# A recurrent head's outputs kept with tokens on partitions, its gate applied at once, and the sample states' decay on ScalarE

## What is computed

```python
h = rms_norm(x, norm1)
u, q, f, i, g = split(h @ w_in)             # 5 parts of 1024 columns
pool_out = pool_mix(u)                      # 4 groups, trailing windows 2, 4, 8, 16
# 8 heads of 128: forget gate F, key 1 - F, query silu(q), value i
F = lb + (1 - lb) * sigmoid(f)
S_t = diag(F_t) S_{t-1} + (1 - F_t)^T v_t   # a 128 x 128 state for each head and sequence
o_t = silu(q_t) S_t
o = rms_norm(o over the head's 128) * hg_norm * silu(g)
x = x + concat(pool_out, o) @ w_o
x = x + (silu(h2 @ w_gate) * (h2 @ w_up)) @ w_down      # h2 = rms_norm(x), width 5632
y = rms_norm(x)
```

## Time and profile before

| | us |
|---|---|
| median of 3 runs | 1520.35 (1520.12 to 1521.35) |
| the profiled execution: its own time | 1519.69 |
| its span, first to last instruction | 1517.9 |
| mean granted clock of TensorE | 0.981 of full speed |
| busy: PE, weight loads, VectorE, ScalarE, GpSimd | 1463.0, 1441.3, 792.6, 560.7, 239.3 |

### The profile page before, as it was taken

How to read it: one execution, slowest core, us unless ns; L and a number is a source line. 1 busy time by engine, 2 the same in 40 slices (tenths; PEclk the granted TensorE clock), 3 DMA queues, 4 the chain that set the end, 5 groups by cost and what they waited for, 6 DMA issues and landing times.

```text
span 1517.9 us, 26905 instructions
## 1 busy us (share of the span) xinstructions
PE 1463.0 (96%) x9816; PEld 1441.3 (95%) x9816; DVE 792.6 (52%) x1214; ACT 560.7 (37%) x831; POOL 239.3 (16%) x410
## 2 busy tenths in 40 slices
PE   7998989889989999999999999999999999999996
PEld 5998988889979999999999999999999999999996
DVE  4556776666755555544444444444444444544443
ACT  6443434434333334333333333333333333333343
POOL 0265345454502220000000000000000000000131
PEclk9999999998989999999999999999999999999998
DMA  8554434445435555554555554556555456555453
GB/s 228 143 133 127 115 97 126 118 134 139 114 100 136 141 152 149 141 154 132 141 162 158 151 153 130 145 149 168 154 139 156 128 145 177 141 155 149 114 142 118
DMA packets 409519, 214.58 MB, mean 141 GB/s; under 512 B 4093, under 2 KB 407757, under 8 KB 409420
## 3 DMA queue, kind: packets, MB, share of 16 engines
q1 hardware_dynamic: 391207, 203.59, 49.2%
q10 hardware_dynamic: 18277, 10.52, 2.4%
HBM read 206.20 MB, written 7.89 MB: 141 GB/s over the span
## 4 chain that ended last, share of the span: by engine, by line
PE 83%; DVE 6%; POOL 4%; issue 3%; ACT 2%; DMA 1%; ACTq 0%; DVEq 0%; POOLq 0%; SPq 0%
PE bank L383 26%; PE bank L384 26%; PE bank L385 26%; POOL km L1555 2%; DVE qr L1224 1%; POOL kp L1564 1%; DVE w_lo L1039 1%; ACT w_hi L695 1%; PE bank L523 1%; DVE sc L1239 1%; DMA xt<-in_x_sample 1%; PE bank L551 0%; PE bank L479 0%; DVE sn L1283 0%; DVE t L1211 0%
## 5 line engine op out<-in xcount | busy, mean ns | idle before, releaser
L383 PE MATMUL bank<-a_hi,w_hi 128*128 128x320 f32 x2048 | 645.4, 315 | 0.0
L384 PE MATMUL bank<-a_lo,w_hi 128*128 128x320 f32 x2048 | 638.9, 312 | 0.0
L385 PE MATMUL bank<-a_hi,w_lo 128*128 128x320 f32 x2048 | 638.7, 312 | 0.0
L1039 DVE TENSOR_TENSOR w_lo<-w_raw,w_hi 128x1024 fp32r<-128x1024 f32 (+1 forms) x416 | 460.0, 1146 | 161.3 <-ACT w_hi L695 159.9
L695 ACT ACTIVATE w_hi<-w_raw 128x1024 fp32r<-128x1024 f32 (+1 forms) x416 | 387.2, 967 | 164.7 <-PE bank L385 137.9
L383 PEld LDWEIGHTS bank<-a_hi,w_hi 128*128 128x128 f32 x2048 | 390.2, 191 | 2.5
L384 PEld LDWEIGHTS bank<-a_lo,w_hi 128*128 128x128 f32 x2048 | 390.4, 191 | 0.8
L385 PEld LDWEIGHTS bank<-a_hi,w_lo 128*128 128x128 f32 x2048 | 390.0, 190 | 0.0
L383 PE MATMUL bank<-h_hi,w_hi 128*128 128x320 f32 x704 | 217.7, 309 | 0.0
L384 PE MATMUL bank<-h_lo,w_hi 128*128 128x320 f32 x704 | 216.5, 308 | 0.0
L385 PE MATMUL bank<-h_hi,w_lo 128*128 128x320 f32 x704 | 216.5, 308 | 0.0
(11 more groups left out here) (228 smaller groups left out, 1245.3 us busy)
## 6 DMA issues: line engine op xcount, KB each, us to landing
w_raw<-in_w_gate SPq DMA_DIRECT2D x44, 1024.0 KB, 5.6
w_raw<-in_w_up SPq DMA_DIRECT2D x44, 1024.0 KB, 5.6
w_raw<-in_w_down SPq DMA_DIRECT2D x64, 704.0 KB, 4.8
w_raw<-in_w_in SPq DMA_DIRECT2D x39, 1024.0 KB, 5.8
w_raw<-in_w_o SPq DMA_DIRECT2D x16, 1024.0 KB, 6.0
s<-in_state_hgrn ACTq DMA_DIRECT2D x8, 512.0 KB, 6.6
out<-sn ACTq DMA_DIRECT2D x8, 512.0 KB, 6.5
xt<-in_x_prompt SPq DMA_DIRECT2D x3, 512.0 KB, 9.2
```

What stands on the lines that cost most here:

```text
L383: pe.matmul(out, whi[:, par_, cols], r_hi, start=(k == 0), stop=False)
L384: pe.matmul(out, whi[:, par_, cols], r_lo, start=False, stop=False)
L385: last = pe.matmul(out, wlo[:, par_, cols], r_hi, start=False, stop=(k == last_k))
L1039: dve.tensor_tensor(wlo[:, par_, cols], raw[:, par_, cols], whi[:, par_, cols].bitcast(F32), SUB)\
```

## The change

Units now come as f q v g for each of the heads 0 to 4 (units `H0` to `L0`), then f q v of heads 5, 6 and 7, then g5 g6 g7. The number of units is the same. A round of the loop is f_{i+1}, q_{i+1}, v_{i+1}, g_{i+1}, four rounds; outputs start four units apart five times, and then twice three.

- `rec_out` has weights and moving side exchanged: `OT` now holds *tokens on partitions*, 128 + 128 + 64, and features as columns. In `rec_s0` a stored state is the moving side (128 columns), and the weights are a window of 32 columns of `qm`, in which only the 8 queries of that sequence aren't zero. `qm` is zeroed once by GpSimd, and VectorE writes the queries into it in `queries` (one product more; the product of level 2 loses its sample columns).
- ScalarE squares `OT` in three instructions with `accum_out`, so the sums over a head's features come out as a column per token block. It takes mean and root, then runs a dummy Silu. VectorE does reciprocal and Newton step. ScalarE scales the three blocks (`rec_scale`), and PE transposes them back (`rec_back`, 3 transposes). `rec_stat`, `rec_bcast`, the diagonals, `osb` and the intermediate split are gone.
- VectorE multiplies the turned output, `hg_norm` and silu(g) in one instruction (`rec_gate`); one split follows. For heads 5 and 6 the turned output is kept in `onb` until their gates exist.
- Silu of q and g is one ScalarE instruction each, in place of sigmoid and a GpSimd product; the forget values use Tanh.
- The decay of the sample states is eight ScalarE copies of 128x128 with a scale per partition (`decayed`); GpSimd keeps `vm`, keys and key copies.
- For the first head VectorE now waits for `sc_zero` ahead of `queries(0)`, and `pool_lo` comes ahead of it.

The diff, cut to what matters. SP's loads follow the new order of units and aren't shown, nor are semaphore names and the removed functions described above.

```diff
+L0 = H0 + 4 * EARLY
+G0 = L0 + 3 * (HEADS - EARLY)
...
+QSTEP = 40
...
             def rec_s0(r):
 
                 pe.wait_ge(s0_loaded, 16 * (r + 1))
-                after(pe, on_ready, r)
-                for b in range(NB):
-                    t = slice(TP + b * TS, TP + (b + 1) * TS)
-                    pe.matmul(OT[:, t], s0[:, b, :], qr[LS][:, t], start=(b == 0), stop=False)
+                pe.wait_ge(qm_ready, r + 1)
+                out = OT[:, TP:TP + P]
+                for i in range(HB):
+                    for j in range(2):
+                        b = HB * j + i
+                        at = QSTEP * b - TS * i
+                        pe.matmul(out[j * HS:(j + 1) * HS, :], qm[:, at:at + HS], s0[:, b, :], start=(i == 0), stop=False)
...
             def rec_out(r):
-                rec_s0(r)
+                if isinstance(r, int) and r > EARLY:
+                    pe.wait_ge(o_kept, r - EARLY)
+                else:
+                    after(pe, gated, r)
                 pe.wait_ge(s1_ready, r + 1)
                 pe.wait_ge(sc_put, PUTS * (r + 1))
-                pe.matmul(OT[:, 0:CH], vt[:, 0, :], sc[:, 0, :], start=False, stop=False)
-                pe.matmul(OT[:, CH:TP], vt[:, 1, :], sc[:, 1, :], start=False, stop=False)
-                pe.matmul(OT[:, CH:TP], s1[:, :], qr[LP][:, CH:TP], start=False, stop=False)
-                pe.matmul(OT[:, TP:N], vt[0:NS, 2, :], scs[:, :], start=False, stop=True).then_inc(o_mm, 1)
+                pe.matmul(OT[:, 0:P], sc[:, 0, :], vt[:, 0, :], start=True, stop=True)
+                pe.matmul(OT[:, P:TP], sc[:, 1, :], vt[:, 1, :], start=True, stop=False)
+                pe.matmul(OT[:, P:TP], qr[LP][:, CH:TP], s1[:, :], start=False, stop=True)
+                rec_s0(r)
+                pe.matmul(OT[0:NS, TP:TP + P], scs[:, :], vt[0:NS, 2, :], start=False, stop=True).then_inc(o_mm, 1)
...
+            def rec_back(r):
+                pe.wait_ge(o_scaled, r + 1)
+                pe.transpose(OT[:, 0:P], tm[:, 0, :], ident)
+                pe.transpose(OT[:, P:TP], tm[:, 1, :], ident)
+                pe.transpose(OT[:, TP:N], tm[0:NS, 2, :], ident[0:NS, 0:NS]).then_inc(o_back, 1)
...
+            def put_out(n, par_, r):
+
+                unit(n, par_, a_rhs, between=(lambda: rec_out(r), None))
+
+            def turned_back(n, par_, r):
+
+                unit(n, par_, a_rhs, between=(None, lambda: rec_back(r)))
...
+            scored(H0 + 3, 1, 0)
+            with pe.Fori(0, EARLY - 1) as i:
+                put_out(H0 + 4 * i + 4, 0, i)
+                turned_back(H0 + 4 * i + 5, 1, i)
+                unit(H0 + 4 * i + 6, 0, a_rhs)
+                scored(H0 + 4 * i + 7, 1, i + 1)
+            put_out(L0, 0, EARLY - 1)
+            turned_back(L0 + 1, 1, EARLY - 1)
+            unit(L0 + 2, 0, a_rhs)
+            for r in range(EARLY, HEADS - 1):
+                n = L0 + 3 * (r - EARLY) + 3
+                scored(n, n % 2, r)
+                put_out(n + 1, (n + 1) % 2, r)
+                turned_back(n + 2, n % 2, r)
+            scored(G0, 1, HEADS - 1)
+            put_out(G0 + 1, 0, HEADS - 1)
+
+            def last_back(k):
+                if k == 12:
+                    rec_back(HEADS - 1)
+            unit(G0 + 2, 1, a_rhs, after_tile=last_back)
...
+                act.activation(zf[:, :], zf[:, :], ACT.Tanh, scale=0.5).then_inc(zf_tanh, 1)
...
+                act.wait_ge(zf_tanh, h + 1)
+                act.activation(tl[0][:, :, 1:3], zf[:, :].rearrange("p (m a) -> p m a", a=2), ACT.Identity,
+                               bias=lbt[:, 3, bass.ds(h, 1)], scale=lbt[:, 5, bass.ds(h, 1)]).then_inc(f_ready, 1)
...
+            def silu_q(h, n):
                 act.wait_ge(unit_read, n + 1)
...
+                act.activation(zq[:, :], zq[:, :], ACT.Silu).then_inc(q_ready, 1)
+
+            def silu_g(g, n):
+                act.wait_ge(unit_read, n + 1)
+                after(act, gm_lo, g)
+                act.activation(ga[:, :], zf[:, :], ACT.Silu).then_inc(g_act, 1)
...
             def rec_squares(r):
                 act.wait_ge(o_mm, r + 1)
...
+                after(act, o_back, r)
+                for i in range(3):
+                    rows = P if i < 2 else NS
+                    last = act.activation(tm[0:rows, i, :], OT[0:rows, i * P:(i + 1) * P], ACT.Square,
+                                          accum_out=oss[0:rows, i:i + 1])
+                last.then_inc(o_squared, 1)
+                act.wait_ge(o_squared, r + 1)
+                after(act, o_rec, r)
+                act.activation(stat[:, 6:9], oss[:, :], ACT.Identity, bias=epst[:, 0:1], scale=1.0 / P)
+                act.activation(stat[:, 0:3], oss[:, :], ACT.Sqrt, bias=epst[:, 0:1], scale=1.0 / P).then_inc(o_std, 1)
+                act.activation(warm[:, 0:1], epst[:, 0:1], ACT.Silu)
+
+            def rec_scale(r):
+                act.wait_ge(newton_step, 4 * (r + 2))
+                for i in range(3):
+                    rows = P if i < 2 else NS
+                    last = act.activation(tm[0:rows, i, :], OT[0:rows, i * P:(i + 1) * P], ACT.Copy,
+                                          scale=stat[0:rows, 3 + i:4 + i])
+                last.then_inc(o_scaled, 1)
+
+            def decayed(r):
+
+                act.wait_ge(s0_loaded, 16 * (r + 1))
+                act.wait_ge(prod_ready, LP * (r + 1))
+                after(act, sn_stored, 16 * r)
+                for b in range(NB):
+                    m = TP // TS // 2 + b // 2
+                    last = act.activation(sn[:, b, :], s0[:, b, :], ACT.Copy, scale=tl[LS][:, m, 1 + b % 2:2 + b % 2])
+                last.then_inc(sdec_ready, 1)
 
...
+            def turn(n, h, r):
+
+                split_hi(n + 1, 1)
+                silu_g(r, n - 1)
                 rec_squares(r)
                 load_s0(h)
                 rec_stores(r)
-                sigmoid_q(h, n + 1)
-                split_hi(n + 3, 1 - par_)
-                rec_std(r)
-                rec_hi(r)
-
-            def gate_window(n, g, h, r):
-
-                split_hi(n + 1, 1)
+                forget(h, n)
+                split_hi(n + 2, 0)
+                rec_scale(r)
+                silu_q(h, n + 1)
+                split_hi(n + 3, 1)
+                gate_split(r)
+                split_hi(n + 4, 0)
+
+            def short_turn(n, h, r):
...
+                split_hi(n + 1, 1 - a)
                 rec_tokens(r)
...
+                decayed(r)
+                forget(h, n)
+                split_hi(n + 2, a)
                 rec_squares(r)
                 load_s0(h)
                 rec_stores(r)
...
+                silu_q(h, n + 1)
+                split_hi(n + 3, 1 - a)
+                rec_scale(r)
...
+            act.activation(warm[:, 0:1], epst[:, 0:1], ACT.Silu)
...
+            split_hi(H0 + 4, 0)
+            rec_tokens(0)
+            decayed(0)
+            with act.Fori(0, EARLY - 1) as i:
+                turn(H0 + 4 * i + 4, i + 1, i)
+                rec_tokens(i + 1)
+                decayed(i + 1)
...
+            n = L0
+            split_hi(n + 1, 1)
+            silu_g(EARLY - 1, n - 1)
+            rec_squares(EARLY - 1)
+            load_s0(EARLY)
+            rec_stores(EARLY - 1)
+            forget(EARLY, n)
+            split_hi(n + 2, 0)
+            rec_scale(EARLY - 1)
+            silu_q(EARLY, n + 1)
+            split_hi(n + 3, 1)
+            gate_split(EARLY - 1)
+            short_turn(L0 + 3, EARLY + 1, EARLY)
+            short_turn(L0 + 6, EARLY + 2, EARLY + 1)
...
+            silu_g(EARLY, G0)
...
+            rec_scale(HEADS - 1)
...
+                                  zq[:, :].rearrange("p (m a) -> p m a", a=2), tl[0][:, :, 1:3], MUL)\
...
+                    n = N if l < LS - 1 else TP
                     dve.wait_ge(qr_ready, (LP + 1) * h + l + 1)
+                    if l == LS - 1:
+                        dve.tensor_tensor(qm[:, :].rearrange("p (b t) -> p b t", t=QSTEP)[:, :, 0:TS]
+                                          .rearrange("p b (a j) -> p b a j", a=2),
+                                          blocks_of(qr[l][:, TP:N], l, NS), times(l, NS, 0, TP), MUL).then_inc(qm_ready, 1)
                     dve.tensor_tensor(blocks_of(qr[l + 1], l, n), blocks_of(qr[l], l, n), times(l, n, 0), MUL)\
...
+            def rec_newton(r):
+                dve.wait_ge(o_std, r + 1)
+                after(dve, o_scaled, r)
+                dve.reciprocal(stat[:, 3:6], stat[:, 0:3]).then_inc(o_rec, 1)
+                dve.wait_ge(o_rec, r + 1)
...
+            def rec_gate(r, src):
+
+                dve.wait_ge(g_act, r + 1)
+                dve.scalar_tensor_tensor(out=ga[:, :], in0=src, scalar=pcol("hg_norm", r), in1=ga[:, :],
+                                         op0=MUL, op1=MUL).then_inc(gated, 1)
+
+            def gate_lo(r):
+                dve.wait_ge(gm_hi, r + 1)
+                split_rest(bh_lo[:, r, :], ga[:, :], bh_hi[:, r, :]).then_inc(gm_lo, 1)
...
```

(81 more changed lines are left out.)

238 lines of the change are left out of this document (43 added, 195 removed).

## The result

The changed kernel takes 1474.72 us (median, 1472.27 to 1478.57), the kernel before 1520.23 in the same comparison: ratio 0.9708, 95% interval 0.9679 to 0.9737. A second comparison gave 1477.51 against 1520.16, ratio 0.9723 (0.9700 to 0.9745). The profiled run took 1473.87 us, its span is 1472.1 (before 1517.9).

The account below looks back on a forecast made before the run. The prediction took the chain of forget values, keys, queries and norm, not PE, as the bound; 19.7 (four-unit windows), 7.1 (three-unit) and 6.3 (tail) made 33.1 us less, forecast 1487 us, range 1478 to 1508.

Parts of the forecast that it names:

- What bounds the kernel: Loop before the last 1063 us: keys on GpSimd, `qq`, query levels and norm close it; shorter PE alone gains nothing.
- Four-unit windows: Five loop windows between output starts: 40 us each (39.2 to 40.8), 200 for 219.71, 19.7 us less.
- Three-unit windows: Two short loop windows: 32 us each (31.2 to 33.5), 64 for 71.07, 7.1 us less.
- PE's own work: PE work inserted between a window's matmuls: falls from 9.9 to 8.0 us, sample products taken as 1.4.
- Tail: Last gate unit, turning back after tile 12: 16.8 us (16 to 17.5) for 23.12, 6.3 less.
- Start: Up to the first output: zeros wait against removed 0.88 us product and earlier `pool_lo`; 0, give or take 1 us.
- Decays cost nothing: Eight scaled copies on ScalarE, 2.2 us in all against 2.15 on GpSimd: hidden while 8 us of cover last.
- 1 (table time): ScalarE between output and forget values: table switches take longer, 16 us come back, 1503 us; chance 0.10.
- 2 (keys gate the scores): GpSimd's keys, stretched beside VectorE's `w_lo`, end 5 us later; 2 us back in each of seven windows, 1501; chance 0.06.
- 3: VectorE's in-order gate, values and score writes hold the loop at 43.9 us; only 13.4 gained, 1507; chance 0.10.
- 5: ScalarE's norm chain takes 10 us after the output; each four-unit window loses 1.3, run slower at 1527; chance 0.07.
- 4: No effect: windows shrink but the time returns as half clock and longer waits, 1518 to 1523; chance 0.04.

Follow-up runs that it names:

- Silu alone: Kernel before the change, with Silu of q and gates made directly by ScalarE (Tanh for forget values) and GpSimd's two products removed: 1492.82 us, ratio 0.9827.
- Newton first: Changed kernel with reciprocal and Newton steps ahead of w_lo and products, scaled copies ahead of w_hi, in four-unit windows only: 1469.67 us, ratio 0.9679.

## Why the prediction was right, and where it was not

The time fell below the range, and the spans say where: 1484.8 forecast (1486.6 less the 1.8 around the span), 1472.1 measured, 12.7 us. The short windows are 6.9 of it, the tail 1.8, the start 3.9, the four-unit windows 0.1. The start's 3.9 us are no failing of the sum: the profile had the early start, the kernel before the late one. With like starts the miss is 8.3 us.

- **What bounds the kernel: right.** Queries behind keys and `qq` closed the loop, not PE. Silu alone shows it from outside: PE's work is unchanged there and the waits at the scores vanish. That a shorter PE would have gained nothing by itself was not tried.
- **Four-unit windows: right, 199.92 for 200.** Its parts too: forget values at 8.3 for 8.6, transposes from 16.25 for 16.7, wait 2.60 to 2.86 for 3.0. That the sum fits to 0.1 us is luck. The spread was wider than the 39.2 to 40.8 given: 38.4 to 38.6 in the two windows without half clock, where PE's own work is 0.6 shorter than summed, and 40.2 to 41.5 in the three with it.
- **Three-unit windows: the failed step.** "32 each" was measured at 28.53, 6.9 us for the two, more than half of the miss. The 32 were PE's 29.2 and two waits, 1.3 us for the turned output and 1.4 for the query levels; neither exists. Newton was to be ready at 14.6 and was at 12.1: the output is whole at 2.2 for 2.6, and the squares took 0.87 us where I had 1.45 (each pair of ACTIVATE and accumulator read starts 0.25 to 0.27 us behind the one before; I had added 0.26 and 0.19 and rounded up). The prediction doesn't split the rest of its 14.6; the rows below show `w_lo` start 1.07 us behind the start of `w_hi`, half way through it. The query levels were to end at 20.7 and ended at 16.0: from Newton to their end 6.1 us were allowed, which fits the 4.97 with GpSimd's decay beside them, in a window from which the change removes the decay; it took 4.0. And the inserted work was 7.4 for 8.0. The run with two more loads puts the real slack at about 0.9 us.

VectorE of the changed kernel in the three-unit window that starts at 337.12 (ScalarE's `w_hi` starts at 344.43):

```profile
345.50 2.61 DVE L1084 TENSOR_TENSOR w_lo<-w_raw,w_hi 128x1024 fp32r<-128x1024 f32 x2 [1.49 <-ACT w_hi L711]
348.04 0.16 DVE L1340 RECIPROCAL stat<-stat 128x3 f32<-128x3 f32 x1
...
349.22 0.49 DVE L1265 TENSOR_TENSOR qr<-zq,t 128x320 f32<-128x320 f32 x1
349.75 1.02 DVE L1275 TENSOR_TENSOR qr<-qr,t 128x320 f32<-128x320 f32 x2
350.80 0.22 DVE L1272 TENSOR_TENSOR qm<-qr,t 128x64 f32<-128x64 f32 x1
350.94 2.25 DVE L1275 TENSOR_TENSOR qr<-qr,t 128x256 f32<-128x256 f32 x5
```

- **PE's own work: right.** The sample products take 0.99 us start to start (1.4 taken, bounds 1.1 and 2.2, so even the lower bound was high); inserted work falls by 30.46 - 28.53 = 1.9 us, the 1.9 summed, though both levels were 0.6 too high (9.3 and 7.4 us by the windows without waits, for 9.9 and 8.0).
- **Tail: 15.03 for 16.8.** The scaled copies were late by 0.96 us instead of 1.8, and no half clock followed.
- **Start: "0, give or take 1" held for the wrong reason.** With like starts it is 140.4 to 141.6 (changed kernel and Newton first) for 140.35 and 141.12. But direct Silu alone brings the first output 4.7 us forward, and the wait for the zeros takes 4 to 5 us back. I had named that wait and set it off against the removed product; the queue in front of the zeros was not priced. It is GpSimd's own: the keys of the first head end at 119.29, the three memsets run from 119.23 to 119.93, and VectorE has waited 6.43 us for them.

```profile
119.96 0.49 DVE L1265 TENSOR_TENSOR qr<-zq,t 128x320 f32<-128x320 f32 x1 [6.43 <-POOL scs L1632]
```

- **Decays cost nothing: right**, and the coverage too: 2.44 us for 2.2, hidden. What I had not seen is that in the kernel before they cost 1.59 us a window where they stood.
- **Rivals.** 1 (table time) falls: two loads of 1.28 us each, by rows and by the run with two more. 2 (keys gate the scores) falls for this kernel: their cover is 3.3 us for 3.2 in a four-unit window and 0.9 in a three-unit one. It is true the moment PE gets 3 us faster (Newton first), and by the mechanism that it named. 3 and 5 fall: no loop at 43.9, ScalarE's norm chain takes 4.3 us from the first square to the dummy Silu's end. 4 falls by the result. The Trainium skill (ScalarE: Activation LUTs, What ACT_TABLE_LOAD costs) gives a switch as 2.66 us with its drain. The measurement differs and decides: each of the 16 loads behind the eight outputs has its user within 0.02 us, and two more of them lengthened PE's wait by 2.46 us and the span by 26.0, where 35 to 40 had been expected by the page's figure.
- **The range's low end**, 1478, was too near: short windows and tail were both sized towards the slow side, 8.7 us together, and the range allowed them 3.6; and no term stood for the start, which differs by 4.4 us between executions of one kernel.

Not tried: the turned output without the other parts, so its 18.2 us include the new order of the units. Open: why half clock follows some waits only.

## What to carry to other kernels

Work that is "off the path" on GpSimd is not free when VectorE has short instructions at the same time: look for one instruction of a group that is four times as long as its neighbours, and at what starts just before it. When two edits shorten the same chain their gains don't add, and the unit of account is the window's own engine content: compute it (here 28.2 + 7.4 us), and every microsecond above it has a name. After removing a wait read the next one in the trace before forecasting the sum: Newton first gave 8.4 us in its five windows alone and 22.1 with the scores reordered. And before two profiles are subtracted, compare their first 35 us: 4.4 us of the first comparison here were the start.
